# A scan step in another order: convolution taps between the chained states, the square sums of y on GpSimd one step later

## The reference, cut to what matters

```python
    xbc = jax.nn.silu(depthwise_causal_conv(full, prm['conv_w'][l], prm['conv_b'][l]))
...
    y, new_ssm = ssd_scan(xs, dt, a_neg, bm, cm, ssm0.astype(f32), front, chunk)
    y = y + prm['d_skip'][l].astype(f32)[:, None] * xs
    y = y.reshape(b, t, D_INNER).astype(h.dtype)
    y = rmsnorm(y * jax.nn.silu(z), prm['ssd_norm'][l])
    ssd_out = y @ prm['w_ssd_branch'][l]
```

## Time and profile before

| | us |
|---|---|
| median of three runs | 2165.03 |
| lowest and highest | 2163.43, 2165.84 |
| the profiled execution | 2164.07 |
| its span in the trace | 2162.3 |
| TensorE busy (matmuls) | 2008.5 |
| GpSimd busy | 1246.0 |
| VectorE busy | 966.3 |
| ScalarE busy | 925.6 |

### The profile page before, as it was taken

One profiled execution on the slowest core, in us unless ns is written; L12 is line 12 of the kernel. 1 busy time (PEld: TensorE's weight loads), 2 busy tenths in 40 slices (PEclk: granted clock), 3 DMA queues, 4 the chain that ended last, 5 costly groups with the idle time before them and its releaser, 6 DMA issues.

```text
span 2162.3 us, 39577 instructions
## 1 busy us (share of the span) xinstructions
PE 2008.5 (93%) x13486; PEld 1972.4 (91%) x13486; DVE 966.3 (45%) x2021; ACT 925.6 (43%) x1354; POOL 1246.0 (58%) x555
## 2 busy tenths in 40 slices
PE   6999978999999997999999998789998999899997
PEld 6999977889899997999889998788888999889997
DVE  3221177777645425221152212777776363352212
ACT  4343355555333434333343333455554234443332
POOL 5667743444366565666666666434444666666675
PEclk9999998999899999999999999999999999999998
DMA  4444422444344443444434444234344444434442
GB/s 162 145 142 155 156 80 91 153 141 151 125 153 145 145 138 97 141 141 155 146 99 144 151 154 138 80 102 152 131 152 143 134 147 136 138 101 141 145 156 103
DMA packets 86328, 292.28 MB, mean 135 GB/s; under 512 B 15728, under 2 KB 15728, under 8 KB 86256
## 3 DMA queue, kind: packets, MB, share of 16 engines
q1 hardware_dynamic: 68544, 249.13, 35.8%
q10 hardware_dynamic: 17712, 42.22, 5.6%
HBM read 269.29 MB, written 22.02 MB: 135 GB/s over the span
## 4 chain that ended last, share of the span: by engine, by line
PE 84%; DVE 9%; DVEq 2%; issue 2%; DMA 1%; ACT 1%; POOL 1%; ACTq 0%; SPq 0%
PE gb L1021 25%; PE gb L1025 23%; PE gb L1024 23%; PE kb L1157 1%; PE gb L1073 1%; DVE gb L747 1%; PE gb L1076 1%; PE gb L1077 1%; DVEq L701 1%; PE kb L1143 1%; PE kb L1135 1%; DVE t_a L696 1%; DVE t_a L815 1%; PE kb L1118 1%; PE kb L1164 1%
## 5 line engine op out<-in xcount | busy, mean ns | idle before, releaser
L354 POOL TENSOR_TENSOR wlo<-wraw,whi 128x1024 fp32r<-128x1024 f32 x474 | 1139.5, 2404 | 829.7 <-ACT whi L429 811.9
L1021 PE MATMUL gb<-ahi,whi 128*128 128x336 f32 x2256 | 745.6, 331 | 21.3 <-ACT bc L496 6.3
L1025 PE MATMUL gb<-ahi,wlo 128*128 128x336 f32 x2256 | 721.7, 320 | 0.0
L1024 PE MATMUL gb<-alo,whi 128*128 128x336 f32 x2256 | 720.6, 319 | 0.0
L429 ACT ACTIVATE whi<-wraw 128x1024 fp32r<-128x1024 f32 x474 | 494.7, 1052 | 183.7 <-PE gb L1021 122.6
L1021 PEld LDWEIGHTS gb<-ahi,whi 128*128 128x128 f32 x2256 | 431.3, 191 | 27.8 <-POOL wlo L354 11.0
L1024 PEld LDWEIGHTS gb<-alo,whi 128*128 128x128 f32 x2256 | 431.6, 191 | 0.0
L1025 PEld LDWEIGHTS gb<-ahi,wlo 128*128 128x128 f32 x2256 | 429.4, 190 | 0.0
L1021 PE MATMUL gb<-bhi,whi 128*128 128x336 f32 x1248 | 395.6, 317 | 4.4 <-DVE blo L975 4.4
L1024 PE MATMUL gb<-blo,whi 128*128 128x336 f32 x1248 | 393.6, 315 | 0.0
L1025 PE MATMUL gb<-bhi,wlo 128*128 128x336 f32 x1248 | 393.2, 315 | 0.0
(11 more groups left out here) (169 smaller groups left out, 2080.6 us busy)
## 6 DMA issues: line engine op xcount, KB each, us to landing
wraw<-wts SPq DMA_DIRECT2D x474, 512.0 KB, 3.7
ssm_o<-tail ACTq DMA_DIRECT2D x32, 576.0 KB, 4.0
st<-ssm_in ACTq DMA_DIRECT2D x32, 512.0 KB, 4.6
x<-x_in ACTq DMA_DIRECT2D x2, 672.0 KB, 5.0
y<-x ACTq DMA_DIRECT2D x2, 672.0 KB, 3.2
pool_o<-tail ACTq DMA_DIRECT2D x2, 540.0 KB, 5.3
tail<-pst_in ACTq DMA_DIRECT2D x2, 480.0 KB, 4.3
conv_o<-cso ACTq DMA_DIRECT2D x48, 13.5 KB, 2.0
```

The source lines that it names most:

```text
L354: pool.tensor_tensor(wlo[:, s, :], wraw[:, s, :], whi[:, s, :].bitcast(F32), ALU.subtract).then_inc(w_lo, 1)
L1021: ins = pe.matmul(gb[bank][:, 0:T], whi[:, slot, w], xh, start=first and j == 0, stop=False)
L1024: pe.matmul(gb[bank][:, 0:T], whi[:, slot, w], xl, start=False, stop=False)
L1025: ins = pe.matmul(gb[bank][:, 0:T], wlo[:, slot, w], xh, start=False, stop=last and j == tiles - 1)
```

## The change

TensorE: the products within the chunk (L1143) signal their end by a new semaphore, `yi_full`. The two products from the chained states (L1164), which stood between the z unit and the state updates, now stand behind the transposes of the next x.

VectorE: the convolution is split into `conv_entry` and four `tap`s; in a scan step the first tap follows the entry, the second and third stand between the chaining of the states and the fourth behind the new addition. That addition adds the skip term to the products within the chunk (`kb[0]`) as soon as `yi_full` allows, and signals `y_read`. The state updates are added ahead of the token products, and these ahead of the rest of y. The low part of y of tile t is made in step t+1 (`low_part`); the sum of squares leaves VectorE. For VectorE and GpSimd the first group is written out, and the loop has two turns.

GpSimd: `sum_y` adds the squares of tile t in step t+1, between the subtraction and the product of the states. ScalarE: the load of the next states stands ahead of the conversion of y and waits for `su_full` as well; the square waits for the sum of the tile before.

```diff
-            def ssd_step(L, t, q, last):
+            def sum_y(L, t):
+
+                pool.wait_ge(sq_done, L * N_SQ + S_Y + t + 1)
+                pool.tensor_tensor(acc[:, :], acc[:, :], sq[:, 0, :], ALU.add).then_inc(y_sum, 1)
+                pool.wait_ge(y_sum, L * KI + t + 1)
+
+            def ssd_step(L, t, q, first, last):
...
+                if not first:
+                    sum_y(L, t - 1)
                 pool.wait_ge(dec_done, L + 1)
...
                 act.activation(zb, zb, ACT.Silu).then_inc(gate_done, 1)
+                if not last:
+                    act.wait_ge(st_dec, L * KI + t + 1)
+                    act.wait_ge(su_full, L * KI + t + 1)
+                    load_states(L, t + 1)
                 act.wait_ge(val_in, L * N_VAL + V_Y + t + 1)
                 act.activation(bhi[:, t, :], zb, ACT.Copy, scale=par[:, L, bass.ds(G_SSD + t, 1)]).then_inc(hi_done, 1)
+                act.wait_ge(y_sum, L * KI + t)
                 act.activation(sq[:, 0, :], zb, ACT.Square).then_inc(sq_done, 1)
-                if not last:
-                    act.wait_ge(st_dec, L * KI + t + 1)
-                    load_states(L, t + 1)
...
                 if not last:
-                    conv(L, 2 * N_GROUPS + t + 1, M0["ssd"] + 2 * t + 1, XS_BANK, pair, 1 - q)
+                    conv_entry(L, nxt, M0["ssd"] + 2 * t + 1, XS_BANK, pair, 1 - q)
+                    tap(L, nxt, XS_BANK, 0)
+                if not first:
+                    low_part(L, t - 1)
...
                 for c, dst in ((1, pst[:, 1, :]), (2, so[:, SEQS * P:SO])):
+                    if not last:
+                        tap(L, nxt, XS_BANK, c)
                     for h in range(2):
...
                 ins.then_inc(p_done, 1)
+                dve.wait_ge(yi_full, kt + 1)
+                dve.scalar_tensor_tensor(t_a[:, 0, :], xs[:, q, :], pcol(L, G_D + t), kb[0][:, 0:T], ALU.mult, ALU.add).then_inc(y_read, 1)
+                dve.drain()
+                if not last:
+                    tap(L, nxt, XS_BANK, CONV_K - 1)
...
-                with dve.Fori(0, N_GROUPS - 1) as g:
+                for j in range(per):
+                    ssd_step(L, j, j, 0, (j + 1) // per, N_GROUPS + (j + 1) // 2, j == 0, False)
+                with dve.Fori(1, N_GROUPS - 1) as g:
...
                 pe.wait_ge(p_done, kt + 1)
-                for c in (1, 2):
-                    c0, n = CHUNKS[c]
-                    ins = pe.matmul(kb[1][:, c0:c0 + n], pst[:, c - 1, :], bc[:, cg, c0:c0 + n], start=True, stop=True)
-                ins.then_inc(y_full, 1)
-
...
                     x_token_major(L, t + 1, 1 - q)
+                for c in (1, 2):
+                    c0, n = CHUNKS[c]
+                    ins = pe.matmul(kb[1][:, c0:c0 + n], pst[:, c - 1, :], bc[:, cg, c0:c0 + n], start=True, stop=True)
+                ins.then_inc(y_full, 1)
```

More of the change, by code:

```diff
@@ L304, in build @@
         p_done = sem("states_chained")
+        yi_full = sem("intra_products_ready")
+        y_sum = sem("square_of_y_summed")
         y_full = sem("y_products_ready")
@@ L405, in _ @@
                 run(L, U0["dt"] + 2, U0["ssd"] + 1)
-                with pool.Fori(0, N_GROUPS - 1) as g:
+                for j in range(TILES_PER_GROUP):
+                    ssd_step(L, j, j % 2, j == 0, False)
+                with pool.Fori(1, N_GROUPS - 1) as g:
                     for j in range(TILES_PER_GROUP):
-                        ssd_step(L, TILES_PER_GROUP * g + j, j % 2, False)
+                        ssd_step(L, TILES_PER_GROUP * g + j, j % 2, False, False)
                 for j in range(TILES_PER_GROUP):
-                    ssd_step(L, KI - TILES_PER_GROUP + j, j % 2, j == TILES_PER_GROUP - 1)
+                    ssd_step(L, KI - TILES_PER_GROUP + j, j % 2, False, j == TILES_PER_GROUP - 1)
+                sum_y(L, KI - 1)
                 run(L, U0["mix"], U0["f2i"])
@@ L726, in out_tiles, with conv_entry @@
                         dve.drain()
-            def conv(L, c, m, bank, pair, side):
+            def conv_entry(L, c, m, bank, pair, side):
                 dve.wait_ge(g_full, L * N_G + m + 1)
@@ L741, in conv, with tap @@
                 dve.drain()
+            def tap(L, c, bank, k):
                 n = CW - HIST
                 cv = gb[bank][:, 0:n]
[L744 to L748, removed]
+                w = pcol(L, G_CW + CONV_K * c + k)
+                if k == 0:
+                    dve.tensor_scalar(cv, xp[:, 0:n], w, None, ALU.mult)
+                elif k < CONV_K - 1:
+                    dve.scalar_tensor_tensor(cv, xp[:, k:k + n], w, cv, ALU.mult, ALU.add)
+                else:
+                    dve.scalar_tensor_tensor(cv, xp[:, k:k + n], w, cv, ALU.mult, ALU.add).then_inc(cv_in, 1)
+            def conv(L, c, m, bank, pair, side):
+                conv_entry(L, c, m, bank, pair, side)
+                for k in range(CONV_K):
+                    tap(L, c, bank, k)
+                    if k < CONV_K - 1:
+                        dve.drain()
             def group_b(g):
@@ L829, in ssd_step @@
                 ins.then_inc(so_done, 1)
-                dve.wait_ge(hi_done, L * N_HI + H_Y + t + 1)
-                dve.wait_ge(sq_done, L * N_SQ + S_Y + t + 1)
-                dve.tensor_tensor(acc[:, :], acc[:, :], sq[:, 0, :], ALU.add)
-                dve.scalar_tensor_tensor(blo[:, t, :], zb, pcol(L, G_SSD + t), bhi[:, t, :].bitcast(F32),
-                                         ALU.mult, ALU.subtract).then_inc(b_done, 1)
+                if not last:
+                    times_dt(L, t + 1)
+                dve.wait_ge(e_exp, kt + 1)
+                dve.wait_ge(y_full, kt + 1)
+                dve.tensor_tensor(yi, yi, eab[:, q, :], ALU.mult)
                 dve.drain()
+                dve.tensor_tensor(t_a[:, 1, :], yi, t_a[:, 0, :], ALU.add)
+                dve.drain()
+                dve.wait_ge(gate_done, L * N_GATE + KF + t + 1)
+                dve.tensor_tensor(zb, zb, t_a[:, 1, :], ALU.mult).then_inc(val_in, 1)
             for L in range(DEPTH):
```

32 lines of the change are left out of this document (16 added, 16 removed).

## The result

The changed kernel takes **2174.93 us** (median of 11 runs, 2164.87 to 2207.75) against 2163.22 for the kernel before (median of 11). The ratio is **1.0047**, 95% interval 1.0030 to 1.0064: slower by half a per cent, where 2154.0 and a gain were forecast.

The account below looks back on a forecast made before the run. TensorE sets the pace, busy 13.89 of 14.87 us a step; a ring through the store's landing, group steps and fixed indices bring 28 steps from 415.4 to 404.3, 11 us less: 2154 us, range 2138 to 2174.

Parts of the forecast that it names:

- What is removed: Transposes' wait for VectorE's addition L817, 0.96 us in 30 cases: 28.8 us would go if nothing took its place.
- The ring: Loop from VectorE's chunk-state copy through SiLU, transposes, gate product and store landing to the next copy: 14.2 us against 14.87.
- the landing: Ring term: time for the store of new states to land, kept at the earlier median of 4.0 us.
- The store's issue: Ring term on ScalarE: from the product with the gate to the issue of the store, 0.67 us.
- the rival with TensorE as the bound: Ring under 13.9 us, so each scan step costs 13.9 to 14.0: 25 us go, 2139; chance 0.2.
- My own rival: Store bunches with a weight load, landing grows to 5.0, looped steps 15.6 us: 2181; chance 0.22 for slower.
- The clock: TensorE's granted clock left as it is: holes same in number, smaller in most steps, larger where a landing is slow.
- the sum of 415.4: Scan steps 0 to 13 of two layers before the change, 24 x 14.87 + 4 x 14.64; forecast 404.3 after.
- Group steps: Copies of B on VectorE, once per four steps, with GpSimd beside them: 1.65 us more per four steps, 0.41 a step.
- Fixed indices: First group of each layer written out, with shorter pauses behind VectorE's copies: a step 0.4 us shorter.
- Behind step 14: Between the last two scan steps nothing booked: TensorE waits 0.7 for token products and some 1.9 for the low part.
- one rival: Layer 0's stretch at clock 0.50 behind step 14 goes away, half of its 18.27 us back: 2145; chance 0.1.

Follow-up runs that it names:

- low part first: Changed kernel with the low part of y of the step before issued ahead of the convolution's entry instead of behind its first tap: 2161.85 us, ratio 0.9991 to the kernel before.
- early store: Changed kernel with ScalarE issuing the store of new states right behind the load of states, before waiting for the gate product: 2133.87 us, ratio 0.9854; repeated 2127.34, 0.9835.

## Why the prediction was wrong

- **What is removed: right.** No wait of the transposes for VectorE is left. What the prediction called a win of 0.96 us in 30 cases was real; the same idle time came back elsewhere (27.9 and 28.8 us).
- **The ring: right in its path, wrong in one term.** All parts but the landing came to 9.69 us, 0.1 under the forecast for such a step (9.8). The store's issue, 0.67 in the sum, came 0.60 to 0.70 behind the gate product in 24 of 32 cases and 0.04 to 0.05 in the last group. With the 4.0 us of the earlier trace rows the ring would be 13.7, as long as TensorE's own 13.67, and the rival with TensorE as the bound would have come true in the written-out groups; in the undisturbed steps it did. The failed term is the landing. I took it from stores that stood beside a load of states and kept it, though the change moves the store beside a weight load. My own rival worked out the distance, some 0.7 us behind that load, and the runs have 0.35 to 0.75 and landings of 5.1 to 5.7. It had the mechanism and got 0.22; its price, 2181, has all steps at the ring's pace, but in the run that isolates it (low part first) 15 of 28 stores land that late, and the time is 2161.85: the gain of 11 us is gone, and no more.
- **The clock: the step that failed outright.** "The clock I leave as it is" prices a hole by its length. With the low part first, holes of 1.05 to 1.99 us numbered 11, and 3.4 us at half clock came with 8 of them, 1.7 us each on top; the five long steps in a row lost 8.5 us each. 6 us of halved clock became 29 and 61. Even for the kernel before the sum of 415.4 was 8 us short of the 423.4 in the trace, where 6 us are halved clock.
- **The low part: not priced.** The prediction follows it only behind step 14. In every step it had moved behind the convolution's entry, and TensorE's z unit waits for it. The row that warned was in the trace before: the entry's copy, 0.18 us, had taken up to 2.14 (the longest stand ahead of the scans; in scan steps at half clock four took 1.0 to 1.2).

```profile
L735 DVE COPY xp<-cst x48: 179/181/2136, 299.6 to 1634.3; 128x24 f32<-128x24 f32 x24, 128x24 f32 x24
```

  This step alone is worth 12 us by the ratios (1.0047 and 0.9991) and turned "no gain" into a loss.
- **Group steps: booked at another place than they cost.** The small copies of group B, for which I took 0.6, take 0.22 and 0.29 as before in all but one case. With late landings the copy of B apart comes behind the state product and takes 1.21 us, in seven of eight cases. But the update products (L1212) wait for it, which the prediction doesn't name: 0.35, 0.68 and 1.56 us in three of the changed kernel's steps. Where the copy does meet the state product (early store), 1.58 of 1.71 us of overlap were lost, not the 0.17 for 0.31 that I took from the earlier trace rows. The Trainium skill (SBUF — State Buffer, Who interferes with whom) says that a VectorE instruction with two SBUF inputs contends with a GpSimd instruction that reads SBUF, and calls the shared ports an exclusive lock; here the trace agrees, with L786 at 2.79 instead of 1.21.
- **Fixed indices: nearly right.** Undisturbed steps last 13.67 us in the unrolled groups and 13.9 to 14.0 in the looped ones, 0.3 apart where I took 0.4; what makes it up was not tested.
- **Behind step 14: as booked in sum.** TensorE waits 1.46 us for the token products and 1.56 for the low part, 3.0 together, where 0.7 and 1.9 were booked and 3.21 stood before. The stretch at 0.50 behind it, which one rival let go away, lasts 6.8 us in layer 0 and 13.7 in layer 1, against 20.5 and 6.8 before. The profiled spans differ from that of before by what the 28 steps differ, within 4 us (low part first: 1.9 and 3.7 shorter; changed: 43.7 and 47.4 longer).
- **The chances.** Slower by over 0.2% had 0.22 for one mechanism. The loss needed two, the landing and the low part, and a clock that multiplies both.

## What to carry to other kernels

When a reorder takes away a short wait on the bounding engine, ask where its idle time goes: here the same sum in fewer and longer holes cost more than many short ones, because the clock came down with them. Price a transfer by what is on its way beside it at its new place, not by the median of its old one. And issue a store as soon as its data is there: moving it ahead of a wait that it didn't need turned a loss of 0.5% into a gain of 1.5%.

## What was not expected of the hardware

- **A wait of 2.1 us that comes back by itself.** One late instruction on VectorE, 17.0 us at half clock with TensorE busy for 16.90 of them, and through the slower x unit the same late instruction in the next step: 23.7 to 24.0 us a step, five in a row.
- **More work, hardly more time.** 18 more matmuls in each scan step, some 60 us in 28 steps, cost 7 us in the run, and its four runs agree within 4 us.
- **A small copy at the price of a large instruction.** 24 columns that take 0.18 us took 2.37, the length of GpSimd's subtraction beside it.
